# Head projections of a hybrid encoder: swapping the halves of the roped rows by transfers between tiles instead of a permutation matmul

## The reference

```python
def apply_rope(x, ang):
    cos = jnp.cos(ang).reshape(shape).astype(x.dtype)
    sin = jnp.sin(ang).reshape(shape).astype(x.dtype)
    x1, x2 = jnp.split(x, 2, axis=-1)
    return jnp.concatenate([x1 * cos - x2 * sin, x2 * cos + x1 * sin], axis=-1)
...
def axial_rope(x, ang_row, ang_col):
    half = HD // 2
    return jnp.concatenate([apply_rope(x[..., :half], ang_row), apply_rope(x[..., half:], ang_col)], axis=-1)
...
    q = axial_rope(rms_norm(zq.reshape(b, s, H_C, HD), c_q_norm), ang_row, ang_col)
    k = axial_rope(rms_norm(zk.reshape(b, s, KV_C, HD), c_k_norm), ang_row, ang_col)
```

## Time and profile before

| | |
|---|---|
| median of 3 runs | 3801.49 us (3800.35 to 3801.64) |
| the profiled execution, own time | 3800.7 us |
| its span, first to last instruction | 3798.9 us |
| TensorE matmul busy | 3667.9 us, 97% of the span |
| VectorE, ScalarE, GpSimd busy | 1858.2, 1567.2, 1158.2 us |
| mean granted TensorE clock | 0.982 of full |

### The profile page before, as it was taken

One profiled execution on the slowest core, in us unless ns is written; L12 is line 12 of the kernel. 1 busy time (PEld: TensorE's weight loads), 2 busy tenths in 40 slices (PEclk: granted clock), 3 DMA queues, 4 the chain that ended last, 5 costly groups with the idle time before them and its releaser, 6 DMA issues. The chain is left out here.

```text
span 3798.9 us, 49840 instructions
## 1 busy us (share of the span) xinstructions
PE 3667.9 (97%) x18289; PEld 3025.5 (80%) x18289; DVE 1858.2 (49%) x2932; ACT 1567.2 (41%) x2504; POOL 1158.2 (30%) x840
## 2 busy tenths in 40 slices
PE   7899999999999999999999999999899999999997
PEld 5678777768888888888767877777687888888886
DVE  5123877983534433333551358689454333434335
ACT  3332877983421112212252348789642122221123
POOL 2133444433522122212242334434333222121213
PEclk9999999999999999999999999999999999999998
DMA  4322221103211111111323223211221111111112
GB/s 142 121 68 74 70 77 27 38 19 114 75 39 39 33 44 39 38 33 39 105 71 125 70 66 82 58 32 27 73 95 40 45 39 39 33 42 36 33 44 111
DMA packets 202443, 227.43 MB, mean 60 GB/s; under 512 B 14751, under 2 KB 162757, under 8 KB 202245
## 3 DMA queue, kind: packets, MB, share of 16 engines
q1 hardware_dynamic: 202285, 225.37, 19.7%
HBM read 173.86 MB, written 51.48 MB: 59 GB/s over the span
## 5 line engine op out<-in xcount | busy, mean ns | idle before, releaser
L237 PE MATMUL ps<-hh,wh 128*128 128x512 f32 (+1 forms) x2736 | 988.2, 361 | 46.8 <-PEq L231 16.9
L238 PE MATMUL ps<-hl,wh 128*128 128x512 f32 (+1 forms) x2736 | 974.1, 356 | 0.0
L239 PE MATMUL ps<-hh,wl 128*128 128x512 f32 (+1 forms) x2736 | 972.8, 356 | 0.0
L2360 POOL TENSOR_TENSOR wl<-raw,wh 128x1024 fp32r<-128x1024 f32 x126 | 301.7, 2401 | 1267.2 <-ACT wh L2197 1267.2
L237 PEld LDWEIGHTS ps<-hh,wh 128*128 128x128 f32 x2736 | 520.7, 190 | 127.7 <-issue 40.6
L238 PEld LDWEIGHTS ps<-hl,wh 128*128 128x128 f32 x2736 | 520.7, 190 | 78.2 <-issue 5.7
L239 PEld LDWEIGHTS ps<-hh,wl 128*128 128x128 f32 x2736 | 520.0, 190 | 73.8
L2421 DVE SCALAR_TENSOR_TENSOR cb<-ps,params,cb 128x1023 f32<-128x1023 f32 (+1 forms) x172 | 144.0, 879 | 870.3 <-ACT cb L2206 870.3
L1467 DVE TENSOR_TENSOR pl<-ps,ph 128x512 fp32r<-128x512 f32 (+1 forms) x576 | 375.6, 653 | 54.7 <-ACT ps L1312 54.3
L1421 DVE TENSOR_REDUCE mx<-ps 128x1 f32<-128x512 f32 x480 | 330.8, 689 | 141.4 <-PE ps L1226 82.7
L1311 ACT ACTIVATE ph<-ps 128x512 fp32r<-128x512 f32 (+1 forms) x576 | 329.7, 572 | 158.6 <-PE ps L1192 153.4
(11 more groups left out here) (242 smaller groups left out, 5613.5 us busy)
## 6 DMA issues: line engine op xcount, KB each, us to landing
raw<-in_w_up SPq DMA_DIRECT2D x88, 512.0 KB, 3.9
heads<-stage SPq DMA_DIRECT2D x38, 640.0 KB, 3.5
raw<-in_w_down SPq DMA_DIRECT2D x44, 512.0 KB, 3.7
rq<-heads SPq DMA_DIRECT2D x56, 320.0 KB, 4.8
raw<-in_w_in SPq DMA_DIRECT2D x32, 512.0 KB, 4.9
rk<-heads SPq DMA_DIRECT2D x32, 320.0 KB, 4.7
raw<-in_w_out SPq DMA_DIRECT2D x16, 512.0 KB, 4.3
residual<-my SPq DMA_DIRECT2D x32, 256.0 KB, 2.0
```

The costliest lines, as they stand in the source:

```text
L237: pe.matmul(out, wh, xh, start=(k == 0), stop=False)
L238: pe.matmul(out, wh, xl, start=False, stop=False)
L239: last = pe.matmul(out, wl, xh, start=False, stop=(k == len(pairs) - 1))
L2360: pool.tensor_tensor(c.wl[slot][:], c.raw[parity][:], c.wh[slot][:].bitcast(F32), ALU.subtract).then_inc(w_lo, units)
```

## The change

The matmul with `perm_c`, its bank and its semaphore go. SyncE issues for each roped unit eight transfers of 16 partitions by 1280 columns from `stage` into `rot`, each to the partner half's partitions (`turn`), ahead of the weight load and the store of the same pass of its loop. VectorE multiplies the whole `rot` by the sine in place, and the sign that the matrix carried goes into the sine table. The sums of squares go to banks 6 and 7 by turns, wait for `squared` in place of `evacuated`, and for the root two blocks back in place of the last one.

```diff
                 for n in range(2, UNITS):
+                    if n - 4 in ROPED:
+                        turn(n - 4)
                     load_weights(sp, c, n, c.raw[n % 2][:], head_unit(c, L, n), raw_arrived, w_lo, 2)
                     if n >= 4:
                         store(n - 4)
...
+                def turn(n):
+                    r = n - ROPED[0]
+                    sp.wait_ge(evacuated, n + 1)
+                    if r >= 2:
+                        sp.wait_ge(roped, r - 1)
+                    for g in range(0, P, 16):
+                        from_row = g + 16 if g % 32 == 0 else g - 16
+                        sp.dma_start(c.rot[n % 2][g:g + 16, :], c.stage[n % 3][from_row:from_row + 16, :]).then_inc(turned[n % 2], 16)
...
-                    pe.wait_ge(evacuated, n + 1)
-                    if 3 * r + b >= 1:
-                        pe.wait_ge(sum_read, 3 * r + b)
-                    pe.matmul(bank(c, 6, w), c.block_ones[:], c.psq[n % 2][:, t0:t0 + w], start=True, stop=True).then_inc(unit_sum, 1)
-                    if 3 * r + b >= 1:
-                        pe.wait_ge(turn_read, 3 * r + b)
-                    pe.matmul(bank(c, 7, w), c.perm_c[:], c.stage[n % 3][:, t0:t0 + w], start=True, stop=True).then_inc(turned, 1)
+                    pe.wait_ge(squared, r + 1)
+                    if 3 * r + b >= 2:
+                        pe.wait_ge(sum_read, 3 * r + b - 1)
+                    pe.matmul(bank(c, 6 + (r + b) % 2, w), c.block_ones[:], c.psq[n % 2][:, t0:t0 + w], start=True, stop=True).then_inc(unit_sum, 1)
...
-                        act.activation(c.pln[:, t0:t0 + w], bank(c, 6, w), ACT.Ln, scale=1.0 / 64, bias=c.eps[:]).then_inc(sum_read, 1)
+                        act.activation(c.pln[:, t0:t0 + w], bank(c, 6 + (r + b) % 2, w), ACT.Ln, scale=1.0 / 64, bias=c.eps[:]).then_inc(sum_read, 1)
...
-                    for b, (t0, w) in enumerate(BLOCKS):
-                        dve.wait_ge(turned, 3 * r + b + 1)
-                        dve.tensor_tensor(rot[:, t0:t0 + w], bank(c, 7, w), c.sin[:, t0:t0 + w], ALU.mult).then_inc(turn_read, 1)
-                    dve.wait_ge(turn_read, 3 * r + 3)
+                    dve.wait_ge(turned[n % 2], 128 * (r // 2 + 1))
+                    dve.tensor_tensor(rot[:], rot[:], c.sin[:], ALU.mult).then_inc(turn_read, 1)
+                    dve.wait_ge(turn_read, r + 1)
...
-        "sin_c": np.tile(np.concatenate([sin_r, sin_r, sin_l, sin_l]), (2, 1)),
+        "sin_c": np.tile(np.concatenate([-sin_r, sin_r, -sin_l, sin_l]), (2, 1)),
```

More of the change, by code:

```diff
@@ L782, in head_projections @@
         w_hi, w_lo, w_used = sem("w_hi"), sem("w_lo"), sem("w_used")
-        tables, evacuated, squared, unit_sum, turned = sem("tables"), sem("evacuated"), sem("squared"), sem("unit_sum"), sem("turned")
+        tables, evacuated, squared, unit_sum, turned = sem("tables"), sem("evacuated"), sem("squared"), sem("unit_sum"), [sem("turned0"), sem("turned1")]
         sum_read, turn_read, root, cos_done, added, roped = (sem("sum_read"), sem("turn_read"), sem("root"), sem("cos_done"),
@@ L828, in _, with norm @@
             def _(pe):
-                def norm_and_turn(n, b):
+                def norm(n, b):
                     r = n - ROPED[0]
                     t0, w = BLOCKS[b]
-                    pe.wait_ge(evacuated, n + 1)
-                    if 3 * r + b >= 1:
-                        pe.wait_ge(sum_read, 3 * r + b)
-                    pe.matmul(bank(c, 6, w), c.block_ones[:], c.psq[n % 2][:, t0:t0 + w], start=True, stop=True).then_inc(unit_sum, 1)
-                    if 3 * r + b >= 1:
-                        pe.wait_ge(turn_read, 3 * r + b)
-                    pe.matmul(bank(c, 7, w), c.perm_c[:], c.stage[n % 3][:, t0:t0 + w], start=True, stop=True).then_inc(turned, 1)
+                    pe.wait_ge(squared, r + 1)
+                    if 3 * r + b >= 2:
+                        pe.wait_ge(sum_read, 3 * r + b - 1)
+                    pe.matmul(bank(c, 6 + (r + b) % 2, w), c.block_ones[:], c.psq[n % 2][:, t0:t0 + w], start=True, stop=True).then_inc(unit_sum, 1)
                 def first_maximum(j):
@@ L844, in first_maximum @@
                         pe.wait_ge(sum_read, 3 * len(ROPED))
-                        pe.wait_ge(turn_read, 3 * len(ROPED))
                     pe.wait_ge(c.q_hi, qt // 4 + 1)
@@ L887, in _ @@
                     if n - 1 in ROPED:
-                        project(pe, c, n % 2, n % 2, lambda b: norm_and_turn(n - 1, b)).then_inc(w_used, 1)
-                        norm_and_turn(n - 1, 2)
+                        project(pe, c, n % 2, n % 2, lambda b: norm(n - 1, b)).then_inc(w_used, 1)
+                        norm(n - 1, 2)
                     else:
@@ L1016, in _ @@
                     first_values(part)
-        end_phase(nc, raw_arrived + [w_hi, w_lo, w_used, tables, evacuated, squared, unit_sum, turned, sum_read, turn_read,
-                                     root, cos_done, added, roped, head0] + stored)
+        end_phase(nc, raw_arrived + [w_hi, w_lo, w_used, tables, evacuated, squared, unit_sum, sum_read, turn_read,
+                                     root, cos_done, added, roped, head0] + stored + turned)
 def attention(nc, c, L):
```

## The result

The changed kernel takes 3779.43 us at the median of 4 runs (3774.71 to 3781.40), beside 3800.97 for the kernel before (4 runs, 3800.35 to 3801.64): a ratio of 0.9941, 95% interval 0.9926 to 0.9956, some 21.5 us less. The profiled execution took 3781.4 us.

The account below looks back on a forecast made before the run. TensorE was taken to bound the head projections. Removing the permutation matmul saves 21.3 us and the hidden transfers cost zero: 3800.7 - 21.3 = 3779.4, against the median 3780.2, forecast 3780 us, range 3777 to 3787.

Parts of the forecast that it names:

- What bounds: Head projections: TensorE, 97% busy, waits only at the barriers before and behind the stage, so every instruction removed saves time.
- E: The moment TensorE ends a unit and ScalarE starts reading its banks; E to E was 18.14 us, forecast 16.0.
- What goes: The permutation matmul's passes on TensorE: 2.13 us a unit, ten units, 21.3 us saved.
- the 0.10 that it left open: Remaining 0.10 us a unit on TensorE, put down to changing between operand kinds; may go or stay, 1.0 us in all.
- Banks and weaker wait: Sums in two banks and their other wait: worth nothing, since TensorE does not wait at these places.
- What is added: On SyncE, eight issues a unit, 4.0 us (3.0 to 5.0), then 3.9 us for the last landing (2.1 to 8.1).
- the prediction's round: From one roped unit to the next through store, issues, landing and VectorE's work: 14.2 us, under the pace of 16.0.
- The weight load behind them: Queued on SyncE behind the transfers, 4.0 us later; read 31 us after issue, so covered; otherwise 4 us a unit.
- The chain: Transfers, sine and addition finish about 1.7 us before the root is ready, cost zero; TensorE has 7.8 us of slack.
- the formula: TensorE's loss a layer for a round of L us: 3L + 8.2 - 64.0 us where above zero, from L = 18.6.
- Rival 1: The eight transfers run one behind the other: slower than before, 3810 us, or 3833 if also behind the store; chance 0.08.
- Rivals 2 and 3: Second: round slightly too long, 18.6 to 22.3 us, time 3783 to 3794, chance 0.07. Third: saving not arriving, about 3800, 0.04.

Follow-up runs that it names:

- e1: The changed kernel without the 80 transfers, the sine multiplying the row itself and the exchange of halves left out: 3781.26 us, ratio 0.9945 to the kernel before.
- e2: The kernel before with only the permutation matmul taken out, no transfers, exchange of halves left out: 3779.24 us, ratio 0.9944.
- e3: The changed kernel with the sums of squares put back into one bank and under the old waits: 3779.67 us, ratio 0.9947.
- e5: The changed kernel with squares and matrix of ones in the projections' operand kind, so each sum is one short pass: 3762.13 us, ratio 0.9900 to the kernel before.
- e4: The changed kernel with each exchange cut into 16 transfers of 8 partitions: 3782.35 us, ratio 0.9951 to the kernel before.
- e6: The changed kernel with each exchange cut into 32 transfers of 4 partitions: 3861.64 us, ratio 1.0161 to the kernel before.

## Why the prediction was right

- **What bounds.** TensorE alone paces the stage: right. Every E is released by TensorE in the changed kernel, in e1, e2, e3 and in e5.
- **What goes, 2.13 us a unit, 21.3 in all.** Right in mechanism and size: 18.14 - 15.97 = 2.17 us a unit, 21.7 over both stages. Where the other 0.04 lies is not shown. Nor do the rows bear out the prediction's reason for the 0.10 that it left open, a cost of changing between kinds of operand: from the start of the sum at 244.60 to that of the second pass behind it, at 245.58, there are 0.98 us, which is the sum's own 0.85 and one pass of 256 columns at 0.12, with 0.01 over. e2 shows that this alone is the gain, and e5 that the sum, which the prediction priced alike, is made of the same passes: without its slow ones a unit loses another 15.97 - 14.36 = 1.61 us, where 1.56 was worked out.
- **Banks and weaker wait, nothing.** Right: from the first E to the end, the stages of e3 and of the changed kernel agree to 0.01 us in both layers.
- **What is added, 4.0 us of issue and 3.9 of landing.** The sum was near, both terms were mis-sized. An issue took 5.33 / 8 = 0.67 us with its gap, not 0.5, more than the dear end of 0.63: without its gap a transfer from tile to tile takes 0.59 at the median and up to 1.33, against 0.34 for the store and 0.58 for the load that I bounded it by the earlier trace rows. The landing behind the last issue took 2.0 us, not 3.9; all 80 landed within 3.5 us of their own issue, so the store just ahead did not visibly hold them up. It is 7.35 us in all, where 7.9 stood. That the two errors nearly cancel is luck, but the forecast did not hang on it: with issues of 0.67 and the 3.9 us of landing, the prediction's round is 15.6 us, still under the pace.
- **The weight load behind them, covered.** Right: it was issued 5.4 us after the store's end instead of 4.0, and nothing waited for it.
- **The chain, 1.7 us of slack to the root and 7.8 to TensorE.** Right: the slack to the root is 2.26 us in unit 3 and 1.07 at the least. For TensorE's slack, e4 lost 1.7 us a layer where the formula with the expected terms asks for 1.9. Two of these terms were off against each other: the later rounds were 17.7 us, shorter than 19.2 (the last product had no GpSimd beside it, 1.49 us), and the first was 21.7. e6 crossed the line at which the change is slower than the kernel before. There 38 + 10 = 48 us a layer were expected, and the stages are 43.0 and 41.7 us longer. In layer 0 the miss is ahead of the last sum, 33.2 for 38: the rounds were 26.9, 26.9 and 27.3 us where 28.6 had been put in, and the first unit was roped 13.4 us after E, not 15.2. With these the formula gives 31.6; that the slower passes behind each wait are the rest is likely, but not shown.
- **Rival 1, one behind the other.** It did not come: 8, 16 and 32 transfers take 7.35, 12.8 and 22.0 us from the first issue to the sine, which is 0.62 to 0.67 us for each plus 2.0 once. The Trainium skill, SBUF — State Buffer, under "Can I just issue two DMAs to hit both halves?" and "The DMA setup-cost knee", has such transfers serialize, each with its fixed 2 us; read strictly, an estimated 22 us for eight. The 2.0 us is there, but paid once, behind the last issue. The measurement decides: what repeats is the issue on SyncE.
- **Rivals 2 and 3** did not come. Issues above 0.6 us, one of the two ways to rival 2, did, but with the short landing no round is over the pace, and the saving arrives whole. The prediction's band for rival 2 does not follow from its own formula: a round of 18.6 to 22.3 us gives 3780 to 3802, not 3783 to 3794.

## What to carry to other kernels

A matmul that only moves rows between partitions costs its passes on the engine that bounds the stage; eight narrow transfers did the same here at no cost in time, and can as long as the whole round (the wait for the queue's turn, 8 x 0.67 us of issue, 2.0 us of landing, what follows) is shorter than the work it runs beside. Work out that round and how far the bounding engine is behind it before cutting a move into pieces: 8 were free, 16 cost 1.7 us a layer, 32 made the kernel slower than before. And count passes by the kind of operand: the remaining sums, held in the short kind, gave another 16 us in the two stages.

## What the runs showed of the hardware that was not expected

- The issue of a transfer from tile to tile takes 0.59 us at the median for 16 partitions, 0.62 for 8 and 0.58 for 4, while the store of 128 partitions to memory takes 0.34. Of the eight's 7.35 us, 5.33 are the queue's own time.
- VectorE next to GpSimd: in e4 the sine's product and the addition took 2.78 and 4.12 us where the same forms take 1.49 alone. GpSimd was busy then with these, from its timeline:

```profile
249.71 2.39 POOL L574 TENSOR_TENSOR wl<-raw,wh 128x1024 fp32r<-128x1024 f32 x1 [9.41 <-ACT wh L569]
252.06 4.20 POOL L966 TENSOR_TENSOR st<-stage,cos 128x1280 f32<-128x1280 f32 x1
```

  VectorE's 2.78 end at 253.45 and its 4.12 at 257.61, 1.35 us behind the end of GpSimd's product at 256.26. The Trainium skill, SBUF — State Buffer, "SBUF: two separate sides", says that the two share a pair of ports under a lock that one of them holds for a whole instruction; these rows agree. So does the 2.91 of the last product before: it ends at 239.24, 1.36 us behind the end of GpSimd's L574, which ran from 235.49 to 237.88. A transfer that lands later can so cost more than its delay: in e4 the round with these two products took 21.7 us, the rounds behind it 17.7.
